# Zeroing a token slot table from a scan stage on ScalarE's queue, not from an attention stage on SyncE's

## What is computed

```python
def trunk_layer(x, mod, norms, mix_params, ffn, ctx):
    ...
    y, ctx_out = token_mixers(h, *mix_params, ctx=ctx)   # scan | attention, then w_out
    x = x + gate1 * rms_norm(y, g_post1)
    h = rms_norm(x, g_pre2) * (1 + scale2) + shift2
    x = x + gate2 * rms_norm(ffn(h), g_post2)

def moe_swiglu(u, router, w_gate, w_up, w_down):
    logits = (u @ router).astype(jnp.float32)
    top_v, top_i = lax.top_k(logits, TOP_K)
    top_w = jax.nn.softmax(top_v, axis=-1)
    ...
    hidden = hidden * combine.astype(u.dtype)[..., None]
    return jnp.einsum('blef,efd->bld', hidden, w_down)
```

## Time and profile before

| | us |
|---|---|
| median of 3 runs | 2518.11 |
| lowest, highest | 2517.38, 2518.68 |
| profiled execution | 2522.26 |
| its span on the core | 2520.5 |
| TensorE busy (share of the span) | 2095.1 (83%) |
| VectorE busy | 1420.4 (56%) |
| ScalarE busy | 896.8 (36%) |
| scan stage of the second layer | about 1322 to 1465 |
| attention stage of the second layer | about 1465 to 1653 |
| router stage's scatter (L1450) | from 1807.4 |

### The profile page before, as it was taken

One profiled execution on the slowest core, in us unless ns is written; L12 is line 12 of the kernel. 1 busy time (PEld: TensorE's weight loads), 2 busy tenths in 40 slices (PEclk: granted clock), 3 DMA queues, 4 the chain that ended last, 5 costly groups with the idle time before them and its releaser, 6 DMA issues. The chain is left out here.

```text
span 2520.5 us, 34510 instructions
## 1 busy us (share of the span) xinstructions
PE 2095.1 (83%) x12291; PEld 1798.9 (71%) x12291; DVE 1420.4 (56%) x2368; ACT 896.8 (36%) x1324; POOL 332.3 (13%) x147
## 2 busy tenths in 40 slices
PE   2797658979599999995896668967589999999993
PEld 1795534869599999995894545867467887887882
DVE  0844865664423112314825865764278878887885
ACT  1311100241411021203302101342178878877882
POOL 0420000021433243311320000030100000000001
PEclk9797879989799999997897779978589999999996
DMA  7214230220222122311204160020399638347354
GB/s 202 71 34 138 101 99 17 85 82 3 67 76 82 53 76 76 91 35 34 79 18 170 69 232 0 1 67 1 130 388 411 251 146 308 131 177 295 118 203 175
DMA packets 214206, 301.89 MB, mean 120 GB/s; under 512 B 52432, under 2 KB 143312, under 8 KB 214096
## 3 DMA queue, kind: packets, MB, share of 16 engines
q1 hardware_dynamic: 187744, 279.28, 31.7%
q10 hardware_dynamic: 23472, 10.57, 1.5%
q0 software_dynamic: 2880, 10.49, 1.1%
HBM read 358.20 MB, written 28.61 MB: 153 GB/s over the span
## 5 line engine op out<-in xcount | busy, mean ns | idle before, releaser
L1792 DVE TENSOR_TENSOR ex_wl<-ex_raw,ex_wh 128x1024 fp32r<-128x1024 f32 x364 | 425.9, 1220 | 56.8 <-ACT ex_wh L1671 52.3
L1671 ACT ACTIVATE ex_wh<-ex_raw 128x1024 fp32r<-128x1024 f32 x364 | 372.0, 1058 | 38.8 <-PE psum L1729 32.5
L1729 PE MATMUL psum<-ex_wh,ex_he_hi 128*128 128x512 f32 (+1 forms) x624 | 242.6, 389 | 5.2 <-DVE ex_wl L1792 5.2
L1729 PE MATMUL psum<-ex_wl,ex_he_hi 128*128 128x512 f32 (+1 forms) x624 | 233.5, 374 | 0.0
L1729 PE MATMUL psum<-ex_wh,ex_he_lo 128*128 128x512 f32 (+1 forms) x624 | 233.1, 374 | 0.0
L1938 POOL TENSOR_TENSOR ex_wl<-ex_raw,ex_wh 128x1024 fp32r<-128x1024 f32 (+1 forms) x60 | 160.4, 2675 | 320.7 <-ACT ex_wh L1924 320.7
L1958 PE MATMUL psum<-h_hi,ex_wh 128*128 128x320 f32 x704 | 161.5, 311 | 16.4 <-POOL ex_wl L1938 14.5
L987 ACT ACTIVATE at_prob<-psum,at_mx 128x640 f32<-128x640 f32 (+1 forms) x80 | 56.7, 708 | 312.5 <-DVE at_mx L1196 312.5
L1958 PE MATMUL psum<-h_hi,ex_wl 128*128 128x320 f32 x704 | 161.0, 310 | 0.0
L1958 PE MATMUL psum<-h_lo,ex_wh 128*128 128x320 f32 x704 | 160.9, 310 | 0.0
L1924 ACT ACTIVATE ex_wh<-ex_raw 128x1024 fp32r<-128x1024 f32 (+1 forms) x60 | 68.4, 1142 | 259.0 <-PE psum L1958 242.4
(11 more groups left out here) (369 smaller groups left out, 4839.8 us busy)
## 6 DMA issues: line engine op xcount, KB each, us to landing
ex_raw<-moe_gate_up SPq DMA_DIRECT2D x286, 512.0 KB
ex_raw<-moe_w_down SPq DMA_DIRECT2D x78, 512.0 KB
x<-moe_w_down SPq DMA_DIRECT2D x65, 512.0 KB
wmod_ssd<-w_mod SPq DMA_DIRECT2D x56, 512.0 KB, 5.9
wmod_at<-w_mod SPq DMA_DIRECT2D x24, 512.0 KB, 4.9
ex_raw<-ffn_w_gate SPq DMA_DIRECT2D x22, 512.0 KB, 3.9
ex_raw<-ffn_w_up SPq DMA_DIRECT2D x22, 512.0 KB, 3.8
ex_raw<-ffn_w_down SPq DMA_DIRECT2D x16, 704.0 KB, 4.7
```

Of the source, the lines that this page charges most:

```text
L1671: act.activation(wh[:, i % RING], raw_of(i), ACT.Copy).then_inc(*hi_done.up(1))
L1729: last = pe.matmul(p.psum[:, 2 + g % 2, 0:width], h[:, k], w[:, i % RING, cols], start=(k == 0 and m == 0), stop=(k == KD - 1 and m == 2))
L1792: dve.tensor_tensor(wl[:, i % RING], raw_of(i), wh[:, i % RING].bitcast(F32), ALU.subtract).then_inc(*lo_done.up(1))
```

## The change

The 18 zero writes leave the attention stage and SP's queue. They are now the first thing that ScalarE does in the second layer's scan stage, ahead of its exponentials, after a wait for GpSimd's fill of a new tile `ssd_zeros` of 128 x 256. Each write reads this tile four times over (`insert_dim` makes a dimension of stride 0), so that a table row of 4 KB is written as four pieces of 1 KB. The bytes written are the same. SP gets a wait for all 18 at the end of the scan stage, so that the tile isn't reused too early. The tile `at_zeros`, its fill and its signal go away. In the first layer the new tile is allocated and nothing else changes.

```diff
--- before.py
+++ after.py
@@ -580,7 +580,7 @@
     p.close_stage()
 
 
-def stage_ssd(p, l, t):
+def stage_ssd(p, l, t, slots=None):
 
     nc, io = p.nc, p.io
     small = p.sig("ssd_small")
@@ -615,6 +615,7 @@
         xbc, z, xst, y = t["xbc"], t["z"], t["xst"], t["y_ssd"]
         dtr = t["dtcq"][:, :, 0:2 * NH]
         mod = Modulation(p, modulation_units(l)[0], 7, own, f"ssd{l}", 8)
+        zeros, zeros_ready = sb("zeros", [P, D // 4]), p.sig("ssd_zeros")
 
         def unit_steps(n):
 
@@ -639,9 +640,21 @@
                         sp.dma_start(io["new_ssm"][0, l, d, 4 * g:4 * g + 4].rearrange("(j h) q n -> (h q) j n", h=2),
                                      stl[:, d, :, g * NS:(g + 1) * NS]).then_inc(*fin_stored.up(16))
                 sp.wait_ge(*fin_stored.at(64))
+                if slots:
+                    sp.wait_ge(slots["cleared"], 16 * (MAX_BLOCKS + 1))
+
+            if slots:
+                @block.gpsimd
+                def _(pool):
+                    pool.memset(zeros[:], 0.0).then_inc(*zeros_ready.up())
 
             @block.scalar
             def _(act):
+                if slots:
+                    act.wait_ge(*zeros_ready.at(1))
+                    for i in range(1, MAX_BLOCKS + 2):
+                        act.dma_start(slots["slots"][i * SL:(i + 1) * SL].rearrange("p (q c) -> p q c", q=4),
+                                      insert_dim(zeros[:], 1, 4)).then_inc(slots["cleared"], 16)
                 act.wait_ge(*small.at(48))
                 act.wait_ge(*dt_pre.at(1))
                 act.activation(e[:], neg[:], ACT.Exp).then_inc(*e_neg.up())
@@ -894,7 +907,7 @@
     p.close_stage()
 
 
-def stage_attention(p, l, t, slots=None):
+def stage_attention(p, l, t):
 
     nc, io = p.nc, p.io
     w_in, gains_in, cache_in = p.sig("at_w_in"), p.sig("at_gains_in"), p.sig("at_cache_in")
@@ -929,7 +942,6 @@
         probT = sb("probT", [P, 2, LAT + PAST])
         mx = sb("mx", [P, 2 * NH, 2])
         total = sb("total", [P, 2, NH])
-        zeros = sb("zeros", [P, D]) if slots else None
         cq, ckr, o = t["dtcq"][:, :, 2 * NH:], t["ckr"], t["o"]
         ck, kr = ckr[:, :, 0:KVR], ckr[:, :, KVR:KVR + ROPE]
 
@@ -960,17 +972,11 @@
                 sp.wait_ge(*kvn.at(TB))
                 sp.dma_start(io["new_ckv"][0, l], ck[:, LB]).then_inc(*new_out.up(16))
                 mod.load(sp)
-                if slots:
-                    sp.wait_ge(*zeroed.at(2))
-                    for i in range(1, MAX_BLOCKS + 2):
-                        sp.dma_start(slots["slots"][i * SL:(i + 1) * SL], zeros[:]).then_inc(slots["cleared"], 16)
                 sp.wait_ge(*new_out.at(32))
 
             @block.gpsimd
             def _(pool):
                 pool.memset(krt[:], 0.0).then_inc(*zeroed.up())
-                if slots:
-                    pool.memset(zeros[:], 0.0).then_inc(*zeroed.up())
 
             @block.scalar
             def _(act):
@@ -2075,9 +2081,9 @@
                     weights = InWeights(p, l, t["qkv_room"], inner)
                     stage_pre_norm(p, l, 0, None, (hi, lo), weights)
                     stage_in_proj(p, l, weights, hi, lo, t)
-                stage_ssd(p, l, t)
+                stage_ssd(p, l, t, slots if l == 1 else None)
                 scan.close()
-                stage_attention(p, l, t, slots if l == 1 else None)
+                stage_attention(p, l, t)
                 stage_out_proj(p, l, t)
             if l == 1:
                 for prefix in ("at_", "win_", "conv_", "ssd_"):
```

## The result

The changed kernel takes 2543.3 us (median of 4 runs, 2539.9 to 2546.0) against 2517.7 us before, a ratio of 1.0098 with a 95% interval of 1.0083 to 1.0112. That is 25.6 us between the medians, slower and clear of noise. The forecast was 2548, with a range of 2533 to 2562. The profiled execution took 2546.04 us, its span 2544.3 us.

A forecast was written before the change was run, and what follows sets the result against it. ScalarE bounds the scan stage's head; 12.2 MB at 380 GB/s, 32.1 us, hold it 29.8 us beyond its slack. With 0 from the attention stage, against a median of 2518.1: 2548 us, range 2533 to 2562.

The forecast's parts named there:

- The chain: Scan stage's head: VectorE and TensorE wait on ScalarE's `e`; delay beyond 1326.7 us moves the stage's end.
- Removal is worth nothing: Attention stage: taking the 18 zero writes off SP gains at most 0.1 us.
- The hand-over: Head of scan stage: 18 DMAs hold ScalarE until its queue has room, making it 29.8 us late.
- SP's loads count in full: Scan stage: eight quarters and four state loads, 4.19 and 0.26 MB, finish before ScalarE is free, however engines divide.
- A fixed number of pieces: ScalarE's queue: pieces, not bytes, fill it; about 1200 to 2048 fit, 1.2 to 2.1 MB, taken as 1.7.
- second rival: ScalarE's queue: bytes or whole DMAs fill it, 4.9 MB outstanding; 19 to 21 us late, 2537 to 2539 us; chance 0.14.
- TensorE's clock: Scan stage: a slow clock after idling could add 0 to 3 us; taken as 0.
- Hand-over without block: ScalarE's empty queue takes all 18 writes; 2.1 to 4.4 us late, 2520 to 2523 us; chance 0.09.
- Bytes or whole DMAs fill the queue: ScalarE's queue: 4.9 MB may be outstanding, as on SP; kernel 2537 to 2539 us; chance 0.14.
- Slow writes in 1 KB pieces: ScalarE's zero writes: at 250 GB/s they make it 40 us late, 2558 us; chance 0.12.
- The attention stage gains: Attention stage gains without the zeros, hand-over fully hidden in the scan stage; below 2513 us; chance 0.01.
- The writes late for the scatter: Zero writes still in flight at the scatter; held impossible, 1361 against 1807 us.

The follow-up runs named there:

- ScalarE's later place: Changed kernel with ScalarE's 18 writes moved behind its SiLU of z, ahead of the first decay exponential: 2516.0 us, ratio 1.0003.
- on SP's queue: Changed kernel with all 18 writes issued by SP behind the last modulation quarter in the scan stage: ratio 1.0001.
- wide tile: Changed kernel with a zero tile of 128 x 1024, each write 128 pieces of 4 KB, same place and queue: 2534.1 us, ratio 1.0072.
- half of the writes: Changed kernel with nine writes left at the head of ScalarE's list, nine issued by SP behind the modulation quarters: 2523.0 us, ratio 1.0016.
- the control: The kernel before, unchanged, measured again: 2518.5 us against 2516.6, ratio 1.0004.
- the GpSimd run: Changed kernel with the 18 writes issued by GpSimd behind its fill instead of by ScalarE: 2527.5 us, ratio 1.0054.

## Why the prediction was right

**The chain.** Read as ScalarE standing in the middle of the stage's head with 4.5 us of slack. Right: with the same writes at ScalarE's later place or on SP's queue the stage takes 144.5 and 142.9 us, about its old length; the changed kernel makes it 26.9 us longer.

**Removal is worth nothing.** Forecast 0 to 0.1 us, measured 0.1 (29.50 against 29.62).

**The hand-over.** The sum's terms against what came:

| term | forecast | measured |
|---|---|---|
| first hand-over after the stage's start | 0.4 us | 0.36 us |
| outstanding at the end of the row | 1.7 MB (1.2 to 2.1) | 2.13 MB |
| moved by both queues until then | 12.2 MB | 11.8 MB |
| rate | 0.38 MB per us | 0.385 to 0.393 |
| row of 18 | 33.9 us | 32.91 us |
| table load of `e`, late | 29.8 us | 28.8 us |
| scan stage's length | +29.8 us | +26.9 us |
| whole kernel | +30 us | +25.6 us |

The mechanism and nearly all of the size are right. The term for outstanding bytes was too small by 0.4 MB, which is 1.1 us, and the rate a little low, 0.7 us. Against that, the engines ran at only 291 GB/s in their first 3.5 us (1328.3 to 1331.8), some 0.9 us. That SP's loads count in full came true with 1 KB pieces; it does not hold "however the engines divide between the queues", since with 4 KB pieces less than half had moved. A fixed number of pieces, from which the 1.7 MB were taken, isn't exact: 2156 packets lay just above the upper of its two bounds.

The time by itself would not have told this forecast from its second rival: 2543.3 us lies at the border of the two bands (2533 to 2543, 2544 to 2553). The row of 32.91 us and the 2.13 MB outstanding, where the rival had 4.9, tell them apart.

**What gave back more.** I let the delay pass through the stage in full and even allowed 0 to 3 us more for TensorE's clock. It came out 1.9 us less in the profile, and the clock gave it instead of taking it. At the second modulation unit VectorE was still 28.7 us late; at the fourth it was 26.9. In between stand 32 matmuls of one line (L717, in the changed kernel L730). First before, then after, with the stretch around them (PEclk, DMA share and GB/s are the last three):

```profile
1385.30 5.82 PE L717 MATMUL psum<-tri,ssd_da 128*128 128x128 f32 x32
...
1382.00:1390.00 8.00, 7.76 (x40) 7.76 (x41) 5.04 (x9) 0.00 (x0) 0.00 (x0) 0.57 0.58 221
```

```profile
1417.66 3.79 PE L730 MATMUL psum<-tri,ssd_da 128*128 128x128 f32 x32
...
1415.70:1423.70 8.00, 6.91 (x60) 6.63 (x60) 6.30 (x14) 0.00 (x0) 0.00 (x0) 1.00 0.73 260
```

They took 5.82 us where the clock was granted at 0.57 and 3.79 us where it was granted in full (2.4 GHz). The full clock stands there in the changed kernel and in three of the experiments (wide tile, GpSimd, half of the writes), the lower one in the others. Why the one or the other is not shown. Between the 26.9 us of one profile and the 25.6 us of the medians lies chance of the kind the control shows (runs of before from 2511.7 to 2520.9 us, and up to 2532.5 beside the later experiments).

**The rivals.** Hand-over without block: no, 32.91 us. Bytes or whole DMAs fill the queue: no, 5.0 MB down to 1.2 MB were outstanding, nine and a half down to two and a half whole writes, by the size of the pieces; but the reading that replaced it, a fixed number of pieces, isn't exact either. Slow writes in 1 KB pieces: no, 385 to 393 GB/s. The attention stage gains: no more than 0.1 us. The writes late for the scatter: no; SP's closing wait cost nothing, since SP waited 42.0 us for VectorE at that end as before.

The Trainium skill ("DMA: Bandwidth & Descriptors", the table on where the fixed 2 us goes) says that one can emit a lot of descriptors before the cost shows. That table stands in the page's section on DMAs issued by GpSimd, while this queue is ScalarE's. The first three hand-overs, 1536 pieces in 2.42 us, are in line with it; 18 writes of 512 pieces are not.

**What the sum left out.** The chain at the stage's head was told without the transposes of the states, which stand ahead of the sums of `da` in TensorE's list and wait for the four state loads. The small vectors were late by 0.7 us, as said. The states came 6 us later than before, and SP hands over the first quarter 5.7 us into the stage instead of 3.3. That they cost nothing holds only because ScalarE was later still; the GpSimd run, with its 4 KB pieces, shows late loads to be worth 10 us by themselves. Here the sum came out right because the longer delay covers the shorter one, not because the shorter one was priced. Whoever took only the block away, by another engine at the same moment, would meet it.

## What to carry to other kernels

A DMA issued from a compute engine costs that engine until its queue has room, and with many small pieces that meant here until 7.3 of 9.4 MB had moved. So the place in the engine's list decides: ahead of work that others wait for it costs the transfer's time, in front of a long wait it costs nothing. Cut a transfer's source narrow only where the issuing engine is idle, since small pieces lengthen the hand-over at equal bytes: fewer of them fit, and beside another busy queue they get a smaller share of the bytes. And ask separately what the burst does to the loads beside it, because taking the block away uncovers that cost.

## What the runs showed of the hardware that was not expected

- What a queue holds is neither a fixed number of pieces nor of bytes: 1033 packets (3.71 MB) on ScalarE's and 1383 (5.01 MB) on SP's at 4 KB, 1529 to 2156 (1.51 to 2.13 MB) at 1 KB, 2466 (1.24 MB) at 512 bytes. No run here settles what is counted.
- Two busy queues moved equal numbers of packets: 676 and 680 in 5 us of the changed kernel, 403 and 407 in 5.5 us of the wide-tile run. The bytes went by the size of their pieces.
- Stores from GpSimd's queue out of the narrow tile moved in as many packets as 4 KB pieces (2592 for 9.44 MB), where ScalarE's took 9504 in pieces of 1 KB.
- A VectorE operation on ten elements per partition took 4.47 us beside a GpSimd subtraction of 4.49 us that began 0.04 us earlier, and VectorE's difference of 1024 elements took 5.39 us instead of 1.23. In that execution the stages from the second output projection to the router took 116.2 us, in the nine others 107.9 to 108.6.
